# A hybrid decoder step on one core: sample tokens beside the prompt's in the moving operand, modulation in six packed pieces, sample attention reordered

## The reference

```python
def _adaln(x, c, norm_g, w_mod, b_mod):
    mod = jax.nn.silu(c) @ w_mod + b_mod            # c: 1 + 8 vectors, w_mod 1024 x 3072
    shift, scale, gate = jnp.split(mod, 3, axis=-1)
    h = _rms(x, norm_g) * (1 + scale[:, None, :]) + shift[:, None, :]
    return h, gate[:, None, :]
...
    (u_h, u_b, u_c, z_a, q, k, v, qi, ki, wi, z_b, g_a, g_b) = _split_proj(h @ w_in)
...
    branch_a = (u_b * conv_out) * jax.nn.silu(z_a)
    branch_b = attend(q, qi, wi, k, v, ki) * jax.nn.silu(z_b)
    merged = jax.nn.sigmoid(g_a) * (branch_a @ w_pa) + jax.nn.sigmoid(g_b) * (branch_b @ w_pb)
    y = x + gate * (merged @ w_out)
```

## Time and profile before

| | |
|---|---|
| median of 3 runs | 3347.12 us (3343.93 to 3347.26) |
| profiled execution, its own time | 3331.04 us |
| its span, first to last instruction | 3329.2 us |
| TensorE matmul busy | 3225.4 us, 97% |
| VectorE, ScalarE, GpSimd busy | 56%, 34%, 27% |
| transfers | 592.37 MB, mean 178 GB/s |

### The profile page before, as it was taken

One profiled execution on the slowest core, in us unless ns is written; L12 is line 12 of the kernel. 1 busy time (PEld: TensorE's weight loads), 2 busy tenths in 40 slices (PEclk: granted clock), 3 DMA queues, 4 the chain that ended last, 5 costly groups with the idle time before them and its releaser, 6 DMA issues.

```text
span 3329.2 us, 45713 instructions
## 1 busy us (share of the span) xinstructions
PE 3225.4 (97%) x17659; PEld 2708.5 (81%) x17659; DVE 1879.5 (56%) x3608; ACT 1138.9 (34%) x2053; POOL 888.5 (27%) x866
## 2 busy tenths in 40 slices
PE   7999999987899999999999999999999999999999
PEld 6888878864778788879887888889888788889987
DVE  2443498012643699005435999436526899957652
ACT  2355443333533422125325221144325422125431
POOL 2346676453450034101210232010210033110011
PEclk9999999999999999999999999999999999999999
DMA  8665567776476455660564555630373455660007
GB/s 238 220 213 202 191 219 252 270 258 224 141 260 203 168 191 198 215 223 22 189 218 139 177 190 200 234 108 14 117 241 131 148 190 192 217 216 11 11 29 239
DMA packets 281016, 592.37 MB, mean 178 GB/s; under 512 B 17725, under 2 KB 199159, under 8 KB 231138
## 3 DMA queue, kind: packets, MB, share of 16 engines
q1 hardware_dynamic: 270434, 551.70, 48.9%
q0 software_dynamic: 10368, 37.75, 3.2%
HBM read 448.93 MB, written 140.47 MB: 177 GB/s over the span
## 4 chain that ended last, share of the span: by engine, by line
PE 90%; ACT 3%; POOL 2%; DVE 2%; DMA 1%; issue 1%; SPq 1%; ACTq 0%; DVEq 0%; POOLq 0%
PE ps L1073 84%; PE ps L1078 7%; POOL BBL L2199 0%; ACT sKPT L872 0%; DVE RS L1659 0%; DMA QU<-q_scratch 0%; POOL WLH L2059 0%; SPq L457 0%; ACT SC L849 0%; ACT sPT L886 0%; DMA WR<-in_w_in 0%; DMA TABLE<-in_page_table 0%; DVE XN L1593 0%; ACT JUNK L655 0%; ACT WLH L645 0%
## 5 line engine op out<-in xcount | busy, mean ns | idle before, releaser
L1073 PE MATMUL ps<-HTH,WLH 128*128 128x512 f32 x4672 | 1504.4, 391 | 0.0
L1073 PEld LDWEIGHTS ps<-HTH,WLH 128*128 128x128 f32 x4672 | 879.1, 188 | 184.0 <-issue 5.0
L1073 PE MATMUL ps<-HTL,WLH 128*128 128x512 f32 x2336 | 911.6, 390 | 0.0
L1792 DVE TENSOR_SCALAR_CACHE_REDUCE JUNK<-SC,SMALL 128x384 bf16<-128x384 f32 (+13 forms) x392 | 579.9, 1479 | 15.8 <-POOL sSC L2126 1.8
L1073 PEld LDWEIGHTS ps<-HTL,WLH 128*128 128x128 f32 x2336 | 439.8, 188 | 85.4
L1902 DVE CUSTOM_DVE_ANT_0 LP<-ps,SC,RQ 128x512 f32<-128x512 f32 (+3 forms) x320 | 201.8, 667 | 300.2 <-PE ps L1073 178.8
L813 ACT ACTIVATE T<-ps 128x512 f32<-128x512 f32 x192 | 114.9, 598 | 722.2 <-PE ps L1073 720.0
L1073 PE MATMUL ps<-V,T 128*128 128x128 f32 x2176 | 286.3, 277 | 7.1 <-ACT T L944 7.1
L2059 POOL TENSOR_TENSOR WLH<-WR,WLH 128x1024 fp32r<-128x1024 f32 x97 | 233.1, 2403 | 216.3 <-ACT WLH L645 216.2
L1073 PEld LDWEIGHTS ps<-V,T 128*128 128x128 f32 x2176 | 263.8, 192 | 11.5 <-ACT T L944 10.2
L1731 DVE SCALAR_TENSOR_TENSOR SC<-T,WI,SC 128x512 f32<-128x512 f32 (+3 forms) x266 | 179.4, 699 | 126.3 <-ACT T L744 125.8
(11 more groups left out here) (325 smaller groups left out, 4553.5 us busy)
## 6 DMA issues: line engine op xcount, KB each, us to landing
WLH<-w_scratch SPq DMA_DIRECT2D x291, 1024.0 KB, 4.9
w_scratch<-WLH SPq DMA_DIRECT2D x97, 1024.0 KB, 6.0
WR<-in_w_in SPq DMA_DIRECT2D x73, 512.0 KB, 4.3
MW<-in_w_mod SPq DMA_DIRECT2D x24, 512.0 KB, 7.1
XN<-in_x_prompt SPq DMA_DIRECT2D x4, 2048.0 KB, 8.0
q_scratch<-QO SPq DMA_DIRECT2D x32, 256.0 KB, 5.5
ma_scratch<-T SPq DMA_DIRECT2D x32, 256.0 KB, 5.6
gb_scratch<-GB SPq DMA_DIRECT2D x32, 256.0 KB, 6.2
```

The source lines that it names most:

```text
L1073: return pe.matmul(out, lhsT, rhs, start=start, stop=stop, **more)
L1792: ins_ = dve.tensor_scalar(JUNK[0:n, 0:row.shape[1]], row, MID[0:n, c:c + 1], 0.0, ALU.is_ge, ALU.add, accum_out=CNT[0:n, c:c + 1])
```

## The change

1. *Tile 0's products.* The sample route over `sRAW` and `PAIR` is gone. Each operand of tile 0 (h, branch a, branch b, merged) is held in two halves of 288 columns, 256 prompt tokens and 32 sample tokens each, and every matmul of a product becomes two, one a half, into two neighbouring PSUM banks: 48 matmuls of 288 columns. ScalarE reads prompt and sample out of the same banks.
2. *Modulation* comes in six pieces of 512 columns (four buffers). SCT has 32 columns, and four matmuls with 32 stationary columns each go to four column groups. Pieces 4 and 5 are computed behind products 1 and 2. The page table's rows are computed on VectorE behind h. SyncE loads x first, and the first three weights between the pieces.
3. *Sample attention.* Values of a group are multiplied one step later, a quarter behind each key transpose; 19 slots for pages, seven gathers issued in the convolution; the last pair ends with three banks in turn; its turn back is behind the first prompt logits, whose Q are loaded and split in the last projections.

The core of the diff:

```diff
@@ products
-            if t == 0:
-                operand = {"pa": sBA, "pb": sBB2, "wo": sMG}.get(n, sHT)
-                b = aux("parts", j)
-                for k in range(KC):
...
-                    ins_ = mm(ps[b][:, 0:2 * P], operand[:, k, :], WLH[j % 3][:, :, k, :], k == 0, k == KC - 1)
-                ins_.then_inc(*s_parts.mark(j))
...
-                mm(out, WH[j % 3][:, k, :], hi[:, k, :], k == 0, False)
-                mm(out, WH[j % 3][:, k, :], lo[:, k, :], False, False)
-                ins_ = mm(out, WL[j % 3][:, k, :], hi[:, k, :], False, k == KC - 1)
+            halves = [(ps[b][:, :], lambda x, k: x[:, k, :])] if t else [
+                (ps[b + e][:, 0:WIDE], lambda x, k, e=e: x[:, k, e, :]) for e in range(2)]
+            for k in range(KC):
+                for p in parts(t):
...
+                for out, of in halves:
+                    mm(out, WH[j % 3][:, k, :], of(hi, k), k == 0, False)
+                for out, of in halves:
+                    mm(out, WH[j % 3][:, k, :], of(lo, k), False, False)
+                for out, of in halves:
+                    ins_ = mm(out, WL[j % 3][:, k, :], of(hi, k), False, k == KC - 1)
...
-                mm(ps[b][:, 0:NS], sRAW[:, 0, :], PAIR[:, :]).then_inc(*product.mark(j, "S"))
@@ modulation (TensorE)
-            for f in range(4 * g, 4 * g + 4):
-                pe.wait_ge(*mw_in[f % 8].at(f))
-                for k in range(KC):
-                    ins_ = mm(ps[b][0:9, (f % 4) * P:(f % 4 + 1) * P], SCT[:, k, :], MW[f % 8][:, k, :], k == 0, k == KC - 1)
+            pe.wait_ge(*mw_in[q % 4].at(q))
+            for k in range(KC):
+                for g in range(4):
+                    ins_ = mm(ps[b][32 * g:32 * g + 32, 0:P], SCT[:, k, :], MW[q % 4][:, k, g * P:(g + 1) * P],
+                              k == 0, k == KC - 1)
@@ sample_attention (TensorE)
+                    after = (u, c + 1) if c < 3 else (u + 1, 0)
+                    late = (u - 1, c - 1) if c else (u - 2, 3)
+                    for x in range(4):
+                        if after[0] in PAIRS:
+                            keys(*after, x)
+                        if late[0] in PAIRS:
+                            values(*late, x)
@@ SyncE
-                if t == 0:
-                    sp.wait_ge(*s_pv.at(PAIRS[-1], 3))
...
-                if t and i == len(PROJ_B) - 4:
+                if i == len(PROJ_B) - 4:
                     load_q(t, 0)
                     load_q(t, 1)
@@ GpSimd
-        def sum_parts(t, j):
-            if t == 0:
-                pool.wait_ge(*s_parts_copy.at(j))
-                pool.tensor_tensor(sRAW[:, 0, :], sRAW[:, 0, :], sRAW[:, 1, :], ALU.add).then_inc(*s_parts_sum.mark(j))
...
-                    for n in range(4):
+                    for n in range(7):
                         gather_pages(n)
```

More of the change, by code:

```diff
@@ L325, in program @@
     kx_in = [signal(f"kx_in{i}", 16) for i in range(2)]
-    pg_in = [signal(f"pg_in{i}", 16) for i in range(16)]
+    pg_in = [signal(f"pg_in{i}", 16) for i in range(19)]
     q_out = [signal(f"q_out{i}", 16) for i in range(2)]
@@ L479, in _ @@
         sp.dma_start(ST16[:, :], ins["state_conv"][0].rearrange("s w d -> (s w) d")).then_inc(*rows_in.mark("all"))
-        for f in range(8):
-            load_mw(f)
         load_x(0)
+        load_mw(0)
+        load_mw(1)
+        load_w(0)
+        load_mw(2)
+        load_w(1)
+        load_mw(3)
+        load_w(2)
         for s in range(NSEQ):
@@ L486, in _ @@
                          allow_slow_non_contiguous=True).then_inc(*table_in.mark(s))
[L487 to L492, removed]
+        load_mw(4)
+        load_mw(5)
         def store_a(t, i):
@@ L859, in sample_attention, with keys @@
         def sample_attention():
-            def keys(u, c):
-                for g in (0, 2):
+            def keys(u, c, groups):
+                for g in groups:
                     act.wait_ge(*s_kt.at(u, c, g))
@@ L904, in sample_attention @@
                         turned(u - 1, c)
-                if u in PAIRS:
-                    for c in (4, 0, 1, 2, 3):
-                        probabilities(u, c)
+                    if c < 3:
+                        keys(u, c + 1, (0, 2))
+                    elif u + 1 in PAIRS:
+                        keys(u + 1, 0, (0,))
+                for c in (4, 0):
+                    probabilities(u, c)
+                if u + 1 in PAIRS:
+                    keys(u + 1, 0, (2,))
+                for c in (1, 2, 3):
+                    probabilities(u, c)
+            for c in (4, 0, 1, 2, 3):
+                turned(PAIRS[-1], c)
         def key_high(t, f):
@@ L1151, in products @@
[L1151 to L1164 removed]
+                        pe.wait_ge(*operand_ready(t, n, k, p))
@@ L1606, in modulate @@
         def modulate(t, steps):
-            for k in steps:
-                dve.wait_ge(*x_mod.at(t, k))
-                if t and k == 0:
-                    dve.wait_ge(*product.at(len(GEMMS) // TILES * t - KC - 1, last_part(t - 1)))
-                dve.tensor_copy(HTH[:, k, :], T[3 + k % 2][:, :]).then_inc(*h_high.mark(t, k, "P"))
             if t == 0:
+                dve.wait_ge(*mod_ready.at("AM"))
                 dve.wait_ge(*x_t.at(t, "S"))
@@ L1619, in modulate @@
                 dve.wait_ge(*xs_mod.at())
-                dve.tensor_copy(sHTH[:, :, :], T[0][:, :].rearrange("p (k t) -> p k t", k=KC)).then_inc(*h_high.mark(t, "S"))
+                dve.tensor_copy(sample_part("H", 0), T[0][:, :].rearrange("p (k e x) -> p k e x", k=KC, e=2)).then_inc(*h_high.mark(t, "S"))
+            for k in steps:
+                dve.wait_ge(*x_mod.at(t, k))
+                if t and k == 0:
+                    dve.wait_ge(*product.at(len(GEMMS) // TILES * t - KC - 1, last_part(t - 1)))
+                dve.tensor_copy(part(t, "H", 0, k, "P"), paired(t, T[3 + k % 2][:, :])).then_inc(*h_high.mark(t, k, "P"))
         def item_a(t, i, j):
@@ L1868, in put, with sum_up @@
                 ins_.then_inc(*s_attn.mark(u))
+            def sum_up(u):
+                dve.wait_ge(*s_exp.at(u, 3))
+                link(dve.tensor_reduce(SUM[:, 0, 0:1], ABS[:, 0:5], AX_X, ALU.add))
+                link(dve.reciprocal(RIN[:, 0, 0:1], SUM[:, 0, 0:1]))
             keys(0, 0)
-            for u in range(len(PAIRS) + 1):
+            for u in PAIRS:
                 for c in range(4):
-                    if u in PAIRS:
-                        largest(u, c)
-                        if c == 3:
-                            largest(u, 4)
-                    if c < 3 and u in PAIRS:
+                    largest(u, c)
+                    if c == 3:
+                        largest(u, 4)
+                    if c == 1 and u >= 2:
+                        put(u - 2)
+                    if c < 3:
                         keys(u, c + 1)
```

469 lines of the change are left out of this document (241 added, 228 removed).

## The result

The changed kernel takes 3273.15 us (median of 4 runs, 3271.7 to 3276.58) against 3346.01 us of before on the same chip (4 runs, 3343.93 to 3347.26): ratio 0.9784, 95% interval 0.9769 to 0.98, 73 us less. 3266 was forecast. The profiled execution took 3271.7 us, its span is 3269.9.

What follows compares the result with a forecast made beforehand. TensorE's own list was taken to bound the kernel. The terms -30 - 10.8 - 6 - 1.3 - 17.4 - 16 = -81.5 us took the profiled 3331.04 to 3249.5, and 16 us to the median gave 3266; 8 in 10 range 3232 to 3303.

Steps and rivals of the forecast that it cites:

- The pace: Tile 0's products: 48 matmuls of 288 columns at 132 ns, 6.34 us a product, -30 us over 96 products.
- the rule in the Trainium skill: Tile 0's products: N/2.4 + 2.5 ns, so 122.5 ns a matmul, -74 us; as a rival 4%, 3222 us.
- the doubled weight loads: Tile 0's products: rival that loads, 24 to 48 a product, no longer overlap, +227 for -30 us, 3523 us; 3%.
- The waits of the sample's route: Tile 0's projections: TensorE's waits at the PAIR matmul go, 1 us stays for a split behind gathers; -10.8 us.
- The start: Opening up to the first product's end: packed modulation pieces, AM at 45 us, first product ends at 62.3; -17.4 us.
- The first wo and pb products: Tile 0 after attention: waits for merged pieces (-6 us) and for the sample's low half (-1.3 us) go.
- the cover of 5.5 us: First wo product: pieces 0 to 6 of prompt and sample run first, 42 matmuls of 0.132 us, hiding the wait.
- The sample attention: Tile 0: steps of 5.6 us in place of 6.77, 13 us over eleven, plus tail and lead-in gains; -16 us.
- the tail's 3.7 us: End of the sample attention: waits of 0.69 us before each of four values, run ahead with three banks; 3.7 us.
- The step from profile to median: Whole kernel: the median lies 16 us above the profiled execution, so 3249.5 us becomes 3266 us.
- the one of the transfers: Rival: start at 294 GB/s (-10) and sample steps held by gathers in turn (-8), 3281 us; 9%.

Runs made afterwards that it cites:

- norm_early: The changed kernel with the norm of tile 1's tokens done behind tile 0's second pb merge and not the fifth: 3269.7 us.
- old_order: The changed kernel with the sample attention's old order (whole chunks of keys and values, 16 slots, four early gathers); early Q loads and paired operand stay: 3284.16 us.
- held: The changed kernel with the page gathers from the thirteenth on held back until the third chunk of keys has been turned: 3277.49 us.
- early4: The changed kernel with four page gathers ahead of the last projections in place of seven: 3276.89 us.
- paced: The changed kernel with each page gather from the eighth on waiting until the one three before has landed, at most three under way: 3276.43 us.
- combined: The changed kernel with Q loads ahead of the weight loads, tile 1's norm moved, and gathers eight to nineteen paced at three under way: 3260.65 us.
- q_first: The changed kernel with three weight loads issued behind the Q loads of units 3, 4 and 5, not all ahead of unit 2's: 3270.12 us.
- q_norm: The changed kernel with the Q loads ahead of the weight loads and tile 1's norm moved, together: 3268.59 us.

## Why the prediction was right, and where its terms were off

I set the changed kernel's profile against the second one of before, since these two are ordinary executions: 3345.1 - 3269.9 = 75.2 us of span.

- **The pace** was right and a little dear: 6.40 us a product where 6.34 was forecast, 133 ns and not 132. 96 products give 24 us of the forecast 30. The estimate of 122.5 ns by the rule in the Trainium skill (TensorE: Matmul & The Clock Gate, Back-to-back issue gap), which the page gives for the isolated matmul, is not what the trace shows. Nor did the doubled weight loads stop overlapping: 48 of 189 ns are 9.1 us, and a product takes 6.40.
- **The waits of the sample's route.** From uh0's start to zb7's start it was 485.07 us in the second profile of before (215.76 to 700.83) and 456.82 after; less 63 products of 0.25 us that leaves 12.5, beside 10.8 forecast. The nearness is in part luck. TensorE's idle time fell by 5.2 us alone (12.07 to 6.84): the 9.0 us of waits for sRAW went, and the split behind seven gathers cost 4.1 us, not 1. The rest is time in which TensorE is busy; the granted clock of the stage was 0.98 before and 1.00 after, and the sum has no term for that.
- **The start** was mis-sized the other way. Up to uh0 26.4 us came off (215.76 to 189.32), 22.4 without the pace; forecast 17.4. Alone it is worth 19.9 by the runs. The first product ended at 61.9 us, forecast 62.3, in steps of 1.64 to 1.66 us, and AM was there at 45.1, forecast 45: the chain held, but AM's time came out by two errors that made up for each other. The fourth piece landed at 40.1 us and not 37.5, so 31 us of transfers were too few (and 5 + 31 is 36, not 37.5); from the end of its matmuls to AM it was 1.6 us and not 3.5. The price of pieces 4 and 5 differs between executions: the two products with them took 11.98 and 8.57 us where those of before had 10.41 and 8.26, with waits of their own, so 1.9 us and not 4.4; but in seven of the ten profiles with the new opening the two took 22.2 to 24.7 us, 3.5 to 6.1 over before. And in its ordinary execution before itself started 1.25 us later.
- **The first wo and pb products** failed in size: -7.3 forecast, some -1.8 found (125.67 to 119.91 us, less 16 products of 0.25). TensorE no longer waits for sMG but for the last MG pieces of the prompt. The step that failed is the cover of 5.5 us, which I had read as if the pieces came when they used to. VectorE, which had tile 1's norm of 10 us right ahead of the last merges, is a part of why they are late: with the norm moved 2.4 of the 3.9 us of waiting stayed (*norm_early*), and what sets those is open.
- **The sample attention**: -16 forecast, 206.81 to 192.80 us found, -13.8 without zb7's own pace; 11.0 by *old_order*. The steps took 5.97 us, so 8.8 us for eleven and not 13, and the other 5.0 us lie in the tail and the lead-in, forecast 3. How they divide I have not measured; the tail's 3.7 us had only four waits of 0.69 us to go by, which are 2.8. ScalarE's wait for Q 2, 3.52 us before, became 6.12, and 5.9 of it reach TensorE.
- **The step from profile to median** was right in its number and wrong in its reason. I carried 16 us over "with the same difference". Every profile without paced gathers has a stall there, but for the first one of before; in *old_order* it is broken up, with TensorE's longest wait 2.97 us while VectorE waits 7.02 us for a late signal. So against its own profile the change shows 59.3 us, and against like executions 75.

The sum, -81.5 against -73, falls short by 6 us of pace, 5 us at pb and wo and 2 us in the attention, with the start 2 to 5 us and the projections' waits 2 us better. No rival happened; the one of the transfers is 3284 by its own terms, 3266 + 10 + 8, and not 3281. What stays open: why TensorE's signals come late under a burst of gathers, and why the first profile of before had none of it with the longest row of gathers of all. That the burst has a part in it is shown by the stall's move (*held*), its growth (*early4*), its absence (*paced*) and its short return behind the unpaced gathers (*combined*). The burst alone isn't enough, by that first profile, and the path on which signal and transfer meet is not known.

## What to carry to other kernels

Compare a profile with the median of its own kernel before taking terms from it: here 11 us of a "difference between two kernels" was one lucky execution, and a second profile of the old kernel showed it at once. The same holds for small gains: 3 us between medians of two sessions were no more than the unchanged kernel moved by. A long row of indirect gathers should be paced by its landings while other engines hand work to each other every microsecond, but only there; at the end of the stage the same pacing makes the pages late. When an edit removes a wait, look for the next user of the same engine or queue: the MG pieces were late in part for a norm, and the Q block for weight loads, that had always stood ahead of them.

## What the runs showed of the hardware

- TensorE's signals to ScalarE and VectorE came 5 to 12 us late in a burst of page gathers, with the transfer engines' share at 1.0 (412 GB/s); with three gathers under way at most (*paced*, share 0.67 to 0.85 from 657 to 686 us) no wait of TensorE in that stretch was over 1.2 us, past a first one of 3.27 us that all the profiles with the paired operand have. The first profile of before had 22 gathers in a row at the same share (1.03 and 415 GB/s from 715 to 725 us) without it.
- In four of the twelve profiles of kernels with the paired operand a stretch of products ran at 6.24 us in place of 6.40 (37 of them in *q_first* and in *norm_early*, 7 in *q_norm*, about two in *early4*): starts 131 and 129 ns apart in turn (132 and 128 in the last two), where otherwise each fourth start comes 140 ns after the one before. Same instructions, same granted clock of 1.00. That is 6 us for 37 products, and may be part of why *q_first*'s profiled run, 3260.71 us, is 9 to 13 us under its others.
- The same modulation piece took TensorE 1.95 us in some executions and 3.64 us in others, when TensorE had waited before it and its clock was at the lower level (piece 4: 1.95 us in the changed kernel, granted clock 1.00 from 70 to 79 us; 3.64 us in *early4*, 0.62).
